# Two transformer blocks on one core: weight splits put off into the second block's output projection, more convolution taps in its input projection, attention masks loaded in two parts

## What is computed

```python
h = rms_norm_2(x, norm1_g)
q, k, v, u = split(h @ w_in)                 # 512, 512, 512, 1024 columns
q, k = rope(rms_norm(q)), rope(rms_norm(k))  # 8 heads of 64
attn = softmax(causal(q k^T / 8)) v
conv = silu(layer_norm(depthwise_causal_conv31(glu(u))))   # 31 taps, 512 channels
x = x + concat(attn, conv) @ w_out           # the output projection
x = x + (silu(rms(x) @ w_gate) * (rms(x) @ w_up)) @ w_down
```

## The kernel before

| unit | weights | first used by group |
|---|---|---|
| 86 | w_out, upper half, columns 0 to 511 | 180 |
| 87 | w_out, upper half, columns 512 on | 182 |
| 88 | w_out, lower half, columns 0 to 511 | 184 |
| 89 | w_out, lower half, columns 512 on | 186 |
| 90, 91 | w_gate, first chunk | 188, 190 |
| 92, 93 | w_up, first chunk | 192, 194 |

## Time and profile before

### The profile page before, as it was taken

The page is one execution under the profiler, slowest core; times in us unless marked ns, Lnnn a source line. Parts: engine busy times, 40 slices in busy tenths (PEclk is TensorE's granted clock), DMA queues, the critical chain, the costliest instruction groups (busy, mean ns, idle before and its releaser), DMA issues.

```text
span 771.5 us, 9633 instructions
## 1 busy us (share of the span) xinstructions
PE 760.8 (99%) x3712; PEld 636.2 (82%) x3712; DVE 582.8 (76%) x945; ACT 408.6 (53%) x555; POOL 49.3 (6%) x42
## 2 busy tenths in 40 slices
PE   8989999999999999999999999999999999999998
PEld 6878899888888888888888887888988888888886
DVE  5698688697757878687778838699857777768584
ACT  7666255456657546545454546764665344353430
POOL 0200000000001500000000005041000000000000
PEclk9999999999999999999999999999999999999999
DMA  9953434454544467665665567655133665655601
GB/s 334 391 175 110 136 110 142 159 168 161 163 164 164 159 204 249 192 216 175 208 205 179 173 207 273 218 172 164 56 110 109 222 215 181 200 184 199 206 13 54
DMA packets 68508, 137.28 MB, mean 178 GB/s; under 512 B 2544, under 2 KB 6256, under 8 KB 67824
## 3 DMA queue, kind: packets, MB, share of 16 engines
q1 hardware_dynamic: 68032, 135.30, 52.6%
q10 hardware_dynamic: 432, 1.38, 0.5%
HBM read 135.48 MB, written 1.05 MB: 177 GB/s over the span
## 4 chain that ended last, share of the span: by engine, by line
PE 85%; DVE 8%; DMA 3%; ACT 2%; SPq 1%; issue 1%; ACTq 0%
PE b L652 19%; PE b L654 18%; PE b L653 18%; PE SS L652 4%; PE SS L654 4%; PE SS L653 4%; DVE wlo L1605 2%; PE TT L621 2%; PE OO L652 2%; PE OO L654 2%; PE OO L653 2%; DMA cs<-in_cst 2%; DVE ca L2128 2%; DMA xr<-in_x 1%; PE b L814 1%; PE SS L761 1%
## 5 line engine op out<-in xcount | busy, mean ns | idle before, releaser
L1605 DVE TENSOR_TENSOR wlo<-raw,whi 128x2048 fp32r<-128x2048 f32 (+2 forms) x119 | 269.9, 2270 | 80.3 <-ACT whi L1144 79.5
L1144 ACT CAST whi<-raw 128x2048 fp32r<-128x2048 f32 (+2 forms) x119 | 222.9, 1878 | 124.4 <-PE b L654 81.9
L652 PE MATMUL b<-whi,Ahi 128*128 128x512 f32 (+2 forms) x520 | 206.7, 398 | 2.9 <-ACT gates L1217 2.4
L654 PE MATMUL b<-whi,Alo 128*128 128x512 f32 (+2 forms) x520 | 199.8, 384 | 0.0
L653 PE MATMUL b<-wlo,Ahi 128*128 128x512 f32 (+2 forms) x520 | 199.1, 383 | 0.0
L652 PEld LDWEIGHTS b<-whi,Ahi 128*128 128x128 f32 x520 | 97.8, 188 | 21.1 <-ACT gates L1217 2.9
L654 PEld LDWEIGHTS b<-whi,Alo 128*128 128x128 f32 x520 | 97.6, 188 | 19.9
L653 PEld LDWEIGHTS b<-wlo,Ahi 128*128 128x128 f32 x520 | 97.9, 188 | 17.8
L1993 DVE STREAM_TRANSPOSE hT<-ust 32x256 f32<-32x256 f32 (+1 forms) x192 | 81.5, 425 | 2.8
L652 PE MATMUL b<-whi,Bhi 128*128 128x512 f32 x154 | 60.5, 393 | 0.1
L654 PE MATMUL b<-whi,Blo 128*128 128x512 f32 x154 | 60.0, 390 | 0.0
(11 more groups left out here) (295 smaller groups left out, 1095.1 us busy)
## 6 DMA issues: line engine op xcount, KB each, us to landing
raw<-in_w_in SPq DMA_DIRECT2D x38, 1024.0 KB, 5.1
raw<-in_w_up SPq DMA_DIRECT2D x16, 1024.0 KB, 5.4
raw<-in_w_dn SPq DMA_DIRECT2D x16, 1024.0 KB, 5.1
raw<-in_w_d SPq DMA_DIRECT2D x11, 1024.0 KB, 5.0
raw<-in_w_g SPq DMA_DIRECT2D x10, 1024.0 KB, 5.0
raw<-in_w_u SPq DMA_DIRECT2D x10, 1024.0 KB, 5.1
raw<-in_w_out SPq DMA_DIRECT2D x8, 1024.0 KB, 5.1
raw<-in_w_br SPq DMA_DIRECT2D x4, 1024.0 KB, 5.0
```

Of the source, the lines that this page charges most:

```text
L652: e.matmul(dst, xh, H[:, kc, c0:ce], start=first and kc == krs[0], stop=False)
L654: ins = e.matmul(dst, xl, H[:, kc, c0:ce], start=False, stop=last and kc == krs[-1])
L1144: e.copy(whi[:, s, 0:m], raw[:, r, 0:m]).then_inc(s_hi, 1)
L1605: e.tensor_tensor(wlo[:, s, 0:m], raw[:, r, 0:m], whi[:, s, 0:m].bitcast(F32), ALU.subtract).then_inc(s_lo, 1)
```

## The change

Three edits. (1) The masks MB, UO and LG (768 columns) are loaded by a DMA of their own with its own semaphore `d_cs0`, one unit earlier; the rest of `cs1` follows where it was. Two of the four stick-breaking heads start a slot later (9 to 10, 15 to 16). (2) Four slots of `timetable2` take two taps more each; the first four rounds of the attention loop take 4 instead of 6. (3) From unit 86 on the splits are put off, at most to two groups ahead of the first use.

```diff
-    for h, a in enumerate((8, 9, 14, 15)):
+    for h, a in enumerate((8, 10, 14, 16)):
...
-    for s, n in ((10, 8), (12, 2), (14, 4), (16, 3), (18, 3)):
+    for s, n in ((10, 8), (12, 4), (14, 6), (16, 5), (18, 5)):
...
+        first = min(groups[t] for t in unit_of if unit_of[t] == i)
+        if i >= unit_of["p2", 4, 1, 0]:
+            g = max(g, first - {unit_of["p2", 4, 1, 0]: 6, unit_of["wo2", 0, 0, 0]: 5}.get(i, 2))
+            if i > unit_of["wo2", 1, 1, 0]:
+                g = max(free_at[i - NSPL], first - 3 - max(0, i - unit_of["u", 0, 0, 0]) // 2)
         g = max([g] + [h + 1 for h in split_after])
+        assert g <= first - 2, (i, g, first)
...
+            if i == NRAW + 3:
+                o = CST["MB"][0]
+                e.dma_start(cs1[:, o:N1], cst_d[:, N0 + o:N0 + N1]).then_inc(d_cs0, 16)
             if i == NRAW + 4:
                 e.dma_start(cst[:, 136:N0], cst_d[:, 136:N0]).then_inc(d_cs1, 16)
-                e.dma_start(cs1[:], cst_d[:, N0:N0 + N1]).then_inc(d_cs1, 16)
+                e.dma_start(cs1[:, 0:CST["MB"][0]], cst_d[:, N0:N0 + CST["MB"][0]]).then_inc(d_cs1, 16)
...
-            w.wait_ge(d_cs1, 32)     # in sc (TensorE) and sm (VectorE)
+            w.wait_ge(d_cs0, 16)
...
-            conv(6 if k < 4 else 4 if k < 8 else 1)
+            conv(4 if k < 8 else 1)
```

More of the change, by code:

```diff
@@ L253, in build @@
     d_xt = [sem(f"d_xt{i}") for i in range(5)]
+    d_cs0 = sem("d_cs0")
     d_x0, d_x1, d_par, d_cst, d_cs1, d_par2, d_tw, d_tw3, d_hp, d_out = [
@@ L1724, in sm @@
         def sm(h):
-            w.wait_ge(d_cs1, 32)
+            w.wait_ge(d_cs0, 16)
             w.wait_ge(s_sz, h + 1)
```

## The result

| kernel | median of its runs | lowest to highest | ratio to before (95%) |
|---|---|---|---|
| before, same chip | 773.39 us (4 runs) | 773.14 to 773.86 | |
| changed | 781.64 us (4 runs) | 781.30 to 782.12 | 1.0106 (1.0089 to 1.0124) |

What follows compares the result with a forecast made beforehand. TensorE, busy 760.8 of 771.5 us, was taken as the bound, so only its holes count: 773.35 - 2.6 (masks) + 2.4 (taps) - 0.9 (attention) + 4.1 (splits) = 776.35, stated as 776.3; range 775.0 to 778.2.

Steps and rivals of the forecast that it cites:

- Hole A: TensorE's 2.6 us wait before group 12, for ScalarE's evacuation behind head 1's passes; forecast to disappear.
- Hole B: TensorE's wait for VectorE's `r1` before the turn in slot 18; forecast to grow from 1.2 to 3.6 us.
- Group 186 waits for unit 89's split behind group 185: Output projection: unit 89's split comes after group 185's residual and gain, so TensorE starts group 186 3.4 us later.
- Group 188 +0.15, group 190 +0.5: Output projection: later splits are late too, costing 0.1 to 0.2 us at group 188 and 0.5 at 190.
- 4.1: Splits put off, output projection: 3.4 + 0.15 + 0.5 + 0.05 us lost by TensorE waiting for late splits.
- The attention stage gives 0.9: Attention stage, 530 to 561 us: VectorE has fewer splits and taps, so TensorE saves 0.9 us, bounds 0 to 1.6.
- the clock falls: Rival: TensorE drops to its lower clock after one or both long holes, 778.0 to 779.8 us; chance 0.08.
- The price of one fall was put at 1.7: Clock rival: lower clock lasting as long as each hole costs half of 3.5 us, 1.7 per hole.
- masks and heads, -2.6: Before group 12: early masks or late head each free ScalarE's evacuation, saving 2.6 us, bounds 0 to 2.6.
- Nothing is taken away in front of `r1`: Slot 18: unit 86's split stays ahead of `r1`, so six taps add their full 2.4 us.
- 4.9: Upper bound of the splits' cost in the output projection, with each later group's wait at its longest.
- the three terms behind hole A: Taps in the input projection +2.4 us, attention stage -0.9, splits put off +4.1.

Runs made afterwards that it cites:

- 8: Two kernels, each the kernel before with half the masks edit: later head slots alone, 772.32 us; masks loaded in two parts alone, 772.52 us.
- filled: Changed kernel plus matmuls nobody reads, 14 before the turn in slot 18 and 13 before group 186: 778.74 us, ratio 1.0067.
- 2: Also called taps_only: the kernel before with only the change's taps: 776.14 us, ratio 1.0039.
- 4: Also called splits_only: the kernel before with only the splits put off, from unit 86 on: 782.12 us, ratio 1.0113.
- 5: Also called splits_86: the kernel before with splits put off from unit 87 on, unit 86 left after group 174: 779.45 us, ratio 1.0073.
- no_taps: Changed kernel with the taps of before, masks and splits still changed: 779.64 us.
- split89: Changed kernel with units 88 and 89 split after groups 181 and 182 instead of 182 and 184: 776.93 us, ratio 1.0045.
- masks_only: The kernel before with only the masks and heads edit: 772.12 us, ratio 0.9983.
- taps_half: The kernel before with four taps more, three of them ahead of `r1`: 774.72 us, ratio 1.0017.
- best_taps: The kernel best with the change's taps added: 772.48 us, ratio 0.9988 to before.
- best: The kernel before with the change's masks and heads, old taps, and splits put off less far (unit 86 after group 177): 770.87 us, ratio 0.9960.

## Why the prediction was wrong

**Right, in place and size.** Hole A goes by ScalarE's order, and each half of the edit does it alone, as the working said (8). Hole B grows to 3.6 us for six taps of 0.4 (3.6 measured). Group 186 waits for unit 89's split behind group 185: +3.4 (3.4 measured). Group 188 +0.15, group 190 +0.5 (0.2 and 0.6). From 185 to the end, without the falls, 4.4 us by the table (filled less before), for 4.1. The attention stage gives 0.9: from group 179 to 180 filled is 1.1 shorter than before (529.00 to 561.52 against 527.32 to 560.93). The taps alone give the same 1.1 (2) and the splits alone 0.6 (4, 5), so putting off the splits gave nothing here that the taps had not given.

**The step that failed: the rival "the clock falls", with its chance of 0.08.** It was the case that came true. The working saw two holes longer than any of before and named the fall, but kept it out of the sum because no row shows one. It said itself that no hole of before is that long; so the trace can't speak against a fall, and its silence was taken for evidence. The changed profile shows half clock behind both, and filled, which has the same waits for VectorE and no idle TensorE in them, shows what the falls cost: 2.9 us at the median, 4.2 trace against trace. Between the two levels of no_taps lie 3.0. The rule was at hand: the Trainium skill, "TensorE: Matmul & The Clock Gate", Part 1, says that an idle TensorE drops to the lower level. The traces agree, but not in every execution: no_taps and splits_86 show the same hole at group 186 without a fall. The price of one fall was put at 1.7, half the length of its hole. Behind group 186 it is 2.8; behind hole B, always 3.6 us long, it is 1.5 (changed), 1.6 (split89) and 2.6 (taps_only), so it doesn't go by the length of the hole.

**A second term mis-sized: masks and heads, -2.6.** It is 2.6 only against an execution that starts early, as the profiled one of before did. In executions in which the clock reaches the higher level late, every group up to 11 is later, and hole A shrinks: group 4 of splits_86 starts at 18.18 (1.6 later) and its hole before group 12 is 0.8 us. Its trace lists that wait (before: 2.4):

```profile
PE b L658 <- ACT gates L1223: 0.7, 1, 0.7
```

Hole A absorbed the late start. That would explain why the runs of before lie within 1.4 us in the first two sets of experiments while masks_only spreads over 2.9. The median gains 1.1 to 1.2, so the sum was 1.4 too low there. The Trainium skill, in Part 1 of the same page, says that the point at which the clock rises at the start differs from run to run; the traces agree in so far as it differs among the fourteen kernels.

**A step that was wrong and cost nothing.** "Nothing is taken away in front of `r1`" held for VectorE; on ScalarE unit 86's later place adds 1.6 us to hole B by itself (4 against 5). In the changed kernel the taps fill that wait, so the hole is 3.6 and not 5.2.

**Bounds that don't come out of the working.** With the later groups at their longest (0.2, 0.5 and 0.4) the splits come to 4.5 us and not to 4.9, and the sum's ends of 775.4 and 777.4 don't follow from the terms' bounds. Neither matters for what failed.

Put together at the medians: 776.3 forecast, +1.4 for the masks, +0.3 in the output projection and -0.2 in the attention stage give 777.8; filled has 778.7. For the profiled executions the sum closes. At group 255 filled is 5.0 us behind before: 2.1 of late start (group 4), less 2.8 gained until group 178, plus 2.4 in hole B, less 1.1 in the attention stage, plus 4.4 from group 185 on. So the three terms behind hole A, forecast at 5.6, came to 5.7. The 0.9 us that the medians leave are of the size of a late start, but the other runs of filled have no trace. The falls are the rest, from 778.7 to the 781.6 measured.

## What to carry to other kernels

Where an edit would make TensorE wait longer than it waits anywhere in the trace, price the fall of its clock in the forecast and not in a rival, and look at several executions, for a hole of the same length is followed by it in one and not in the next. A hole early in the program may be paying for a late start: what closing it gives at the median is found over executions with both starts. Put a split off only as far as what VectorE waits for ahead of it leaves room, and look at its rounding on ScalarE as well.

## What the runs showed that I had not expected

- After idle times of 3.14 us (group 186) and 3.4 us (hole B) the granted clock was half for the next stretch in the profiles of changed, taps_only, splits_only and split89, but not behind group 186 in those of no_taps (by its starts) and splits_86, whose hole there is the same 3.4 us from start to start.
- After 2.8 us (hole B of splits_only and no_taps), 2.7 us (hole A of taps_half) and 2.6 us (hole A of before) the profiles show no fall. What makes six of ten runs of taps_half, and now and then one of before, have a clock of 0.998 is open, so the runs don't show that holes of this length are safe.
- The start takes up to 2.6 us more or less (group 4 at 16.56 in taps_half, 16.59 in before, 18.88 in no_taps, 19.19 in best_taps), for the most part by when the matmuls change from 0.43 to 0.23 us apart. In best it is the wait for the first rounded weights instead, which is 1.1 us longer than in before.
